# Up projection of a two-block transformer kernel: nine of eleven iterations form one chunk's eight block products as seven, and the opening puts its high products ahead of the low parts

## The reference

```
def conv_gated_mlp(u, w_up, conv_w, conv_b, w_down):
    up = u @ w_up                                   # 2048 -> 2 * 5632
    pad = jnp.pad(up, ((0, 0), (CONV_WIDTH - 1, 0), (0, 0)))
    up = conv_b + sum(pad[:, j:j + S] * conv_w[j] for j in range(CONV_WIDTH))
    gate, val = jnp.split(up, 2, axis=-1)
    return (jax.nn.gelu(gate, approximate=True) * val) @ w_down
```

## Time and profile before

| | |
|---|---|
| median of 3 runs | 2382.51 us |
| profiled execution, its own time | 2382.83 us |
| its span, first to last instruction | 2381.1 us |
| matmul busy | 2368.0 us, 99% of the span, 10776 matmuls |
| DVE, ACT, POOL busy | 1741.2, 1271.9, 186.6 us |
| granted TensorE clock | 0.999 |
| up phase | 11 iterations, from about 460 to 940 us |

### The profile page before, as it was taken

The page is one execution under the profiler, slowest core; times in us unless marked ns, Lnnn a source line. Parts: engine busy times, 40 slices in busy tenths (PEclk is TensorE's granted clock), DMA queues, the critical chain, the costliest instruction groups (busy, mean ns, idle before and its releaser), DMA issues.

```text
span 2381.1 us, 28274 instructions
## 1 busy us (share of the span) xinstructions
PE 2368.0 (99%) x10776; PEld 1964.8 (83%) x10776; DVE 1741.2 (73%) x1579; ACT 1271.9 (53%) x1203; POOL 186.6 (8%) x204
## 2 busy tenths in 40 slices
PE   9999999999999999999999999999999999999998
PEld 8888888888888888888888888888888888888886
DVE  6877645656666666878766565567999999897866
ACT  5544554655665656545545454445555555554535
POOL 5000000001212222000000000001011010000000
PEclk9999999999999999999999999999999999999999
DMA  7566555487887887877698864777777777887874
GB/s 257 193 195 212 168 172 197 165 304 244 256 254 243 263 255 243 289 260 252 215 317 279 263 192 160 223 247 249 234 224 243 240 231 252 280 277 241 270 250 156
DMA packets 278443, 563.57 MB, mean 237 GB/s; under 512 B 14234, under 2 KB 48976, under 8 KB 277712
## 3 DMA queue, kind: packets, MB, share of 16 engines
q1 hardware_dynamic: 277904, 561.53, 72.3%
q10 hardware_dynamic: 448, 0.79, 0.1%
HBM read 512.97 MB, written 50.07 MB: 236 GB/s over the span
## 4 chain that ended last, share of the span: by engine, by line
PE 97%; ACT 1%; DMA 1%; DVE 1%; issue 0%; SPq 0%; POOL 0%; DVEq 0%; POOLq 0%; ACTq 0%
PE ps L1797 22%; PE ps L1799 22%; PE ps L1798 22%; PE ps L1951 8%; PE ps L1953 8%; PE ps L1952 8%; PE ps L1790 2%; PE ps L1791 1%; PE ps L2165 1%; DMA g_work<-turned_rows 0%; PE ps L1773 0%; ACT w_hi L1091 0%; PE ps L2180 0%; DMA turned_rows<-g_work 0%; DVE w_lo L2363 0%
## 5 line engine op out<-in xcount | busy, mean ns | idle before, releaser
L2363 DVE TENSOR_TENSOR w_lo<-raw,w_hi 128x2048 fp32r<-128x2048 f32 x424 | 979.6, 2310 | 589.3 <-ACT w_hi L1091 585.6
L1091 ACT ACTIVATE w_hi<-raw 128x2048 fp32r<-128x2048 f32 x424 | 813.2, 1918 | 1025.5 <-PE ps L1799 662.5
L1797 PE MATMUL ps<-w_hi,xa 128*128 128x512 f32 x1616 | 631.7, 391 | 0.0
L1799 PE MATMUL ps<-w_hi,xa 128*128 128x512 f32 x1616 | 629.1, 389 | 0.0
L1798 PE MATMUL ps<-w_lo,xa 128*128 128x512 f32 x1616 | 628.9, 389 | 0.0
L1797 PEld LDWEIGHTS ps<-w_hi,xa 128*128 128x128 f32 x1616 | 303.4, 188 | 66.4 <-DVE w_lo L2363 3.2
L1799 PEld LDWEIGHTS ps<-w_hi,xa 128*128 128x128 f32 x1616 | 303.4, 188 | 63.3
L1798 PEld LDWEIGHTS ps<-w_lo,xa 128*128 128x128 f32 x1616 | 303.5, 188 | 61.9
L1797 PE MATMUL ps<-w_hi,g 128*128 128x512 f32 x704 | 275.5, 391 | 0.3 <-DVE w_lo L2363 0.3
L1799 PE MATMUL ps<-w_hi,g 128*128 128x512 f32 x704 | 274.0, 389 | 0.0
L1798 PE MATMUL ps<-w_lo,g 128*128 128x512 f32 x704 | 273.9, 389 | 0.0
(11 more groups left out here) (450 smaller groups left out, 2363.8 us busy)
## 6 DMA issues: line engine op xcount, KB each, us to landing
raw<-in_w_in_dram SPq DMA_DIRECT2D x94, 1024.0 KB, 5.4
raw<-in_ffn_w_dram SPq DMA_DIRECT2D x92, 1024.0 KB, 5.8
raw<-in_w_up_dram SPq DMA_DIRECT2D x88, 1024.0 KB, 6.2
raw<-in_w_down_dram SPq DMA_DIRECT2D x44, 1024.0 KB, 6.0
raw<-in_ffn_w_dram SPq DMA_DIRECT2D x80, 512.0 KB, 4.7
raw<-in_w_out_dram SPq DMA_DIRECT2D x32, 1024.0 KB, 5.2
raw<-in_w_pg_dram SPq DMA_DIRECT2D x16, 1024.0 KB, 7.3
raw<-in_pl_w_gate_dram SPq DMA_DIRECT2D x16, 1024.0 KB, 8.4
```

Of the source, the lines that this page charges most:

```text
L1091: A(w_hi[j % SPLIT][:, :], raw[s][:, :], ACT.Copy).then_inc(sem("w_hi_ready"), 1)
L1797: mm(o, high, hi, start=begin, stop=False)
L1799: return mm(o, low, hi, start=False, stop=end)
L2363: V.tensor_tensor(w_lo[j % SPLIT][:, :], raw[j % RAW][:, :], w_hi[j % SPLIT][:, :].bitcast(F32), ALU.subtract).then_inc(sem("w_lo_ready"), 1)
```

## The change

Weight chunks in the up phase's iterations 1 to 9 are dealt out anew. Row tiles 0 to 11 of each half stay plain (chunks 0, 2, 3 gate, 5, 6, 7 value). Tiles 12 and 13 of both halves make chunk 1, tiles 14 and 15 of both make chunk 4, each loaded by two DMAs of 512 KB. Chunk 1 is multiplied as seven block products (21 matmuls, in banks 4 to 7 besides 0 to 2), chunk 4 as eight. Iterations 0 and 10 stay as they were.

```diff
+UP_SEVENS = 9
+UP_SEVEN = 1
+UP_PLAIN = {0: (0, 0), 2: (0, 1), 3: (0, 2), 5: (1, 0), 6: (1, 1), 7: (1, 2)}
+UP_PAIR_TILE = {1: 12, 4: 14}
...
+            def up_early_sums(i):
+                dve.wait_ge(sem(f"raw_landed{UP_SEVEN}"), pairs_landed("up", i, UP_SEVEN))
...
+                V.tensor_tensor(up_sums[:, 0:1024].rearrange("p (k n) -> p k n", k=2), blocks[:, 1],
+                                raw[UP_SEVEN][:, 0:1024].rearrange("p (k n) -> p k n", k=2), ALU.subtract).then_inc(sem("sums"), 1)
+            def up_late_sums(i):
...
+                V.tensor_tensor(r[:, 512:1024], r[:, 1536:2048], up_sums[:, 0:512], ALU.subtract).then_inc(sem("sums"), 1)
+                dve.wait_ge(sem("sums"), up_seven_no(i) * 3 + 2)
+                V.tensor_tensor(up_sums[:, 1024:1536], r[:, 1024:1536], r[:, 512:1024], ALU.subtract).then_inc(sem("sums"), 1)
+            def up_low_sums(i):
+                dve.wait_ge(sem("sums_high"), up_seven_no(i) + 1)
+                V.tensor_tensor(up_sums_low, up_sums, up_sums_high.bitcast(F32), ALU.subtract).then_inc(sem("sums_low"), 1)
...
+            def up_merge(i, gr):
...
+                    V.tensor_tensor(up_summand(gr, a), up_summand(gr, a), bank(2 * gr + a), ALU.add).then_inc(sem("products_merged"), 1)
+            def up_step(j):
...
+                    if j == 0:
+                        earlier_tap(0, 1)(i)
+                    if j == 1:
...
+                        earlier_tap(0, 2)(i)
+                    if j == 2:
...
+                            up_product_sums(i)
+                            up_last_product(i)
+                    if j == 3 and sevens:
+                        up_merge(i, 0)
...
+                    if j == 3:
+                        earlier_tap(1, 1, range(2))(i)
+                    if j == 4 and sevens:
+                        turn_up(i, 0)
+                    if j == 4:
+                        earlier_tap(1, 1, range(2, 4))(i)
+                    if j == 5:
+                        earlier_tap(1, 2)(i)
+                        if more:
+                            up_early_sums(i + 1)
+                    if j == 6 and more:
+                        up_late_sums(i + 1)
+                    if j == 6 and sevens:
+                        up_merge(i, 1)
+                    if j == 7:
+                        if more:
+                            up_low_sums(i + 1)
+                        turn_up(i, 1)
```

```diff
+                if up_seven:
+                    act.wait_ge(sem("sums"), up_seven_no(i) * 3 + 2)
...
                 A(w_hi[j % SPLIT][:, :], raw[s][:, :], ACT.Copy).then_inc(sem("w_hi_ready"), 1)
+                if up_seven:
+                    act.wait_ge(sem("sums"), up_seven_no(i) * 3 + 3)
+                    A(up_sums_high, up_sums, ACT.Copy).then_inc(sem("sums_high"), 1)
```

POOL's five operations an iteration are the same and in the same order; once, in iteration 0, it makes the sums of the factor blocks. In the opening PE multiplies the high weights of tile 0 (chunk 0) and of tiles 0 and 1 (chunk 1) before it waits for their low parts, the third group of x is rounded in two pieces with a signal each, and two products of a block of ones with itself stand ahead of everything:

```diff
+                                if j < 2 and k == 0:
+                                    for k_, n in itertools.product(range(j + 1), range(4)):
+                                        columns_high(0, n, k_, x[:, x0 + k_, :], hi, (j, k_) == (0, 0))
+                                    pe.wait_ge(sem("first_half_low"), 3 * j + 1)
...
+            dve.wait_ge(sem("x_first_high"), 3)
+            x_low_part(8, "x_first_low")
+            dve.wait_ge(sem("factor_high"), 3)
+            x_low_part(10, "factor_ready")
```

More of the change, by code:

```diff
@@ L115, in stream_plan @@
         uses = [len(range(s, body, RAW)) for s in range(RAW)]
-        twice = [GLU_SEVENS * sum(c % RAW == s for c in GLU_PAIR_TILE) * (name == "glu") for s in range(RAW)]
+        pairs = {"up": (UP_SEVENS, UP_PAIR_TILE), "glu": (GLU_SEVENS, GLU_PAIR_TILE)}.get(name, (0, {}))
+        twice = [pairs[0] * sum(c % RAW == s for c in pairs[1]) for s in range(RAW)]
         back = [[2 * RAW] * body for _ in range(2)]
@@ new lines, in up_pair_products @@
+            def up_pair_products(i, hi, lo):
+                for gr, a in itertools.product(range(2), range(2)):
+                    if (gr, a) == (1, 1):
+                        up_bank_free(i, 1, 1)
+                    for k in range(2):
+                        c = slice(512 * (2 * k + gr), 512 * (2 * k + gr + 1))
+                        last = by_rows(2 * gr, xa[:, UP_PAIR_TILE[4] + k, :], hi[:, c], lo[:, c], (gr, a, k) == (1, 1, 0), (gr, k) == (0, 1), a)
+                    if (gr, a) == (0, 1):
+                        last.then_inc(sem("half_multiplied"), 1)
+                return last
@@ L2096, in embedding @@
                         turn(turned, 0)
+            pe.wait_ge(sem("dve_order"), 1)
+            for n in range(2):
+                mm(bank(n % 2)[:, 0:P], part[:, 0:P], part[:, 0:P], start=True, stop=True)
             pe.wait_ge(sem("ident_ready"), 2)
@@ L2540, in slab @@
                 return tiles(ap[:, bass.ds(i * 2048 + gr * 1024, 1024)])
+            then(V.memset(part[:, 0:P], 1.0))
             for b, (m_, of) in enumerate(((modulo, ident[:, :]), (mirrored_modulo, mirror))):
@@ L2927, in turn_up, with convolve @@
                 last.then_inc(sem("blocks_turned"), 1)
-            def convolve(i, gr, tap):
-                for n in range(4):
+            def convolve(i, gr, tap, of=range(4)):
+                for n in of:
                     if tap == 1:
@@ L2938, in convolve, with earlier_tap @@
                                            ff_out[gr][:, n, tap:S], ALU.mult, ALU.add).then_inc(sem(f"up_conv{gr}"), 1)
[L2940 to L2946 removed]
+            def earlier_tap(gr, tap, of=range(4)):
+                return lambda i: None if isinstance(i, int) and i == 0 else convolve(i - 1, gr, tap, of)
@@ new lines, in up_merge @@
+            def up_merge(i, gr):
+                dve.wait_ge(sem("products_read"), i * 3)
+                for a in range(2):
+                    if gr and a:
+                        dve.wait_ge(sem("chunks_multiplied"), chunk_no("up", i, 7) + 1)
+                    else:
+                        dve.wait_ge(sem("half_multiplied"), i * 2 + (UP_HALVES + 1 + gr))
+                    V.tensor_tensor(up_summand(gr, a), up_summand(gr, a), bank(2 * gr + a), ALU.add).then_inc(sem("products_merged"), 1)
@@ L2948, in early_sums @@
+            stream("up", peel=1, started=True, at={j: up_step(j) for j in range(8)}, tail=2)
             def early_sums(ph, c):
```

257 lines of the change are left out of this document (205 added, 52 removed).

## The result

The changed kernel takes 2395.22 us (median of 6 runs, 2394.72 to 2396.79), the kernel before 2382.97 (6 runs, 2382.31 to 2383.66): ratio 1.0053, 95% interval 1.0042 to 1.0063. It is 12.3 us slower; 2395.0 us was predicted. The profiled execution took 2396.79 (span 2395.0), 1.6 above the median.

A forecast was written before the change was run, and what follows sets the result against it. The prediction took PE's matmuls as the bound (97% of the chain), with DVE-POOL exclusion making `w_lo` late. 2382.83 + 13.6 (up phase) - 1.1 (opening) = 2395.3, less 0.3 to the median: 2395.0 us; 8-in-10 range 2381 to 2400.

The forecast's parts named there:

- PE, -6.1: Up phase: 3 matmuls less in each of 9 iterations, 27 x 0.2267 = 6.1 us gained.
- Place 1: Iteration start: early sum delays POOL's product and so `w_lo`; PE waits 0.9 us behind eight boundaries, 7.4 us.
- The drag: Follows from place 1: `w_lo` of chunk 2 comes 0.1 us late, 7 x 0.1 us.
- Place 2: `w_lo` of chunk 3, late behind taps and two POOL operations: 7 x 1.6 = 11.2 us, 0.45 in iteration 2.
- Up phase: Sum of PE's gain, both places and the drag: +13.6 us.
- Opening: Kernel start: first product at 8.58, chunk 1 without its wait, chunk 2 near 22.5; 1.1 us gained.
- The zero terms: Split DMAs, SP's puts, form sums of x in iteration 0 and the two products of ones: each zero.
- 12 us before that: Chunk 1's buffer is free 12 us before the early sum at step 5 wants it, so DMAs cost zero.
- Products from PSUM: DVE products from PSUM and transposes taken as not held by POOL; if held, 0.3 us an iteration at most.
- range of 2389 to 2399: The forecast's own range for the kernel's time, from the bounds of places 1 and 2, iterations alike.
- nothing bites: Rival: no waits arise, the 6.1 and 1.1 us gains are kept, 2375.3 us; chance 0.15.
- L1042 behind `w_lo`: Rival: at place 2 L1042 falls behind `w_lo`, halving the loss: +6.3 - 1.1, 2387.7 us; chance 0.15.

The follow-up runs named there:

- spread_2: Changed kernel with early sum at step 4 (iteration 0: step 5), half 0's taps two, four, two at steps 0 to 2, DVE's loop starting one iteration later: 2377.64 us.
- up_only: The up projection as changed, the opening as in the kernel before: 2396.83 us, ratio 1.0059 to the kernel before.
- no_ones: The changed kernel without filling `part` with ones and without the two products of ones at the start: 2394.61 us, ratio 1.0052.
- again: The changed kernel once more, unedited: 2395.69 us, ratio 1.0051 to the kernel before.
- opening_only: The kernel before with the opening as changed and the up projection untouched: 2381.73 us, ratio 0.9996.
- form_low_filled: Changed kernel with POOL's low part of the forms of u mostly replaced by a zero fill in iterations 2 to 8 (output incomplete): 2388.48 us, ratio 1.0022.
- low_on_dve_ahead: Changed kernel with the product's low part moved from POOL to DVE, early sum at step 4, DVE's loop starting one iteration later: 2378.04 us, ratio 0.9980.
- taps_back: The changed kernel with the taps of half 0 back at steps 1 and 2, as in the kernel before: 2386.17 us, ratio 1.0014.
- early_sum_ahead: The changed kernel with the early sum at step 4 instead of step 5, in iteration 0 too: 2394.29 us, ratio 1.0049.

## Why the prediction was right

The time was met (2395.0 against 2395.22), and the mechanism of both places is shown. That the time fits to 0.2 us is in part luck: the terms below are off by up to 0.9 us each and cancel. Term by term:

- **PE, -6.1.** An undisturbed iteration takes 42.92 us (`spread_2`), 0.60 less than before where 0.68 was counted: -5.4 over nine. Right but for 0.08 an iteration.
- **Place 1, 7.4.** 7.6 in the trace (0.93 six times and 0.99 twice); moving the early sum alone takes the iteration from 45.33 to 44.40. The stated cause, POOL kept waiting for 0.93 us, is the row of 3.31 against 2.41.
- **The drag, 0.7.** Not seen in iterations 3 to 9, for which it was counted; chunk 2 was late once, by 0.2 us, in iteration 2. The first late sum came when forecast (729.63, issue) and the rest was 0.1 us quicker than the hand-laid order.
- **Place 2, 11.2 + 0.45.** 10.3 for the seven (six near 1.47, one of 1.55), and 0.46 in iteration 2. The mechanism was right in each part: L1075 (L1017 before) stretched the taps by 2.16 (2.2 forecast), L1100 (L1042 before) stood ahead of `w_lo` for 1.06 (1.04). The 0.13 too much lie in the times around them: the taps began 0.37 before PE's chunk 2 (740.20), not 0.2.
- **Up phase, +13.6.** 13.1 in the trace from w_hi 79 to 181 (13.0 in `up_only`, 13.7 and 13.8 in `no_ones` and `again`, which have the late transfer). The terms as measured give -5.4 + 7.6 + 0.2 + 10.3 + 0.5 = 13.2.
- **Opening, -1.1.** Nine traces (with `no_ones`) show -1.1 to -1.3 at w_hi 11, but the changed kernel's own two -0.5 and -0.7, and `opening_only` nothing, since x came in late. So for this kernel's own traces the term was about half a microsecond too large: the first product came at 9.17, not near 8.6, since PE's transposes were slow until then, which the sum had not reckoned with. Chunk 1 came without a wait and 0.43 earlier, as said; chunk 2 came at 23.30 instead of 23.74, not at 22.5. Its first trace alone would have read +0.45 at the end of the mixer: 0.3 of x landing later and 0.6 of a slower pace until 93 us, which is not the kernel's.
- **The zero terms.** The split DMAs and the form sums of x show as no wait of PE in iterations 0 and 1, and leaving out the products of ones gained or lost nothing that shows. One has a limit: "12 us before that" holds in the loop, not in iteration 0, where the chunk landed 0.8 us behind the early sum's turn. A step earlier cost 3.3 us of PE.

Products from PSUM were taken as not held, with 0.3 an iteration as the other end. The merges last as long beside POOL's small operations (1.27) as beside nothing (1.28): not held.

```profile
731.36 1.27 DVE L3184 TENSOR_TENSOR g_work<-g_work,ps 128x512 f32<-128x512 f32 x2
...
756.96 1.28 DVE L3184 TENSOR_TENSOR h<-h,ps 128x512 f32<-128x512 f32 x2
...
730.97 0.79 POOL L1092 TENSOR_TENSOR g_work<-g_work,ff 128x128 f32<-128x128 f32 x1
731.84 0.46 POOL L1094 TENSOR_TENSOR g_work<-ff,g_work 128x128 f32<-128x128 f32 x1
```

Two smaller things were off without weight. POOL's small operations take 0.46 us, not the 0.3 estimated. And the range of 2389 to 2399 does not follow from the bounds given for it: nothing at place 1 alone makes 2387.6, and both upper ends together 2400.

The rival "nothing bites" was the better guess for the kernel's idea, not for its order: the same PE work and the same DVE work in another order come near it (2377.6 against 2375.3). "L1042 behind `w_lo`" (+5.2) is in effect what `form_low_filled` made by leaving L1042's work out, +5.6; in the changed kernel's order it did not happen once in seven iterations.

## What to carry over

Two-input operations of POOL and DVE on SBUF shut each other out here, so one long operation of POOL costs a waiting DVE up to its whole length (2.16 us of 2.41 in the taps), and it enters at the first gap in DVE's row: check what DVE issues in the 0.2 us behind the instruction that POOL waits for. To place more work on DVE, put it where a `w_lo` has reserve ahead of that gap, or move POOL's operation to DVE, where it takes half as long (1.22 us against 2.41). A change that frees PE time is judged by the order around it: here the same products were worth +13.1 us, or -3.5 in `spread_2` and -5.1 in `low_on_dve_ahead` (w_hi 79 to 181). And read one-off landings in iteration 0 before moving a use of loaded data forward.

## What the runs showed that I had not expected

`by_columns` pairs (512 and 256 columns) run at one of two paces in the stretch from 24 to 90 us, 2% apart, and the pace is not the kernel's. ACT's `w_hi` rows, each released by PE, sixteen pairs apart, in `taps_back` and `early_sum_ahead`, whose programs are alike up to the up phase:

```profile
57.02 1.92 ACT L1158 ACTIVATE w_hi<-raw 128x2048 fp32r<-128x2048 f32 x1 [3.63 <-PE ps L1907]
62.57 1.92 ACT L1158 ACTIVATE w_hi<-raw 128x2048 fp32r<-128x2048 f32 x1 [3.63 <-PE ps L1907]
```

```profile
57.53 1.91 ACT L1158 ACTIVATE w_hi<-raw 128x2048 fp32r<-128x2048 f32 x1 [3.74 <-PE ps L1907]
63.18 1.92 ACT L1158 ACTIVATE w_hi<-raw 128x2048 fp32r<-128x2048 f32 x1 [3.73 <-PE ps L1907]
```

5.55 us a chunk (0.3467 a pair) and 5.65 (0.3533), at a granted clock of 1.00 in both. Eleven of the fourteen traces have the first, the changed kernel's, `opening_only` and `early_sum_ahead` the second; it is 1.0 us of the kernel's time. The first trace of the changed kernel and its second differ in it, so the program does not set it; what does, no run here shows.
